# Head norms of two attention branches: squares summed as a rounded part and a remainder

## The reference, cut to what matters

```python
def rms_norm(x, g):
    xf = x.astype(jnp.float32)
    y = xf * lax.rsqrt(jnp.mean(xf * xf, axis=-1, keepdims=True) + EPS)
    return (y * g.astype(jnp.float32)).astype(x.dtype)

# in hybrid_layer, run for two layers; 4 heads of 64 in each branch
na = merge_heads(neighbourhood_attention(rms_norm(split_heads(nq, NA_HEADS), na_q_norm_g),
                                         rms_norm(split_heads(nk, NA_HEADS), na_k_norm_g),
                                         split_heads(nv, NA_HEADS), na_rpb))
mk, mv = jnp.split(rms_norm(mem, norm_mem_g) @ w_mem_kv, 2, axis=-1)
mo = merge_heads(memory_attention(rms_norm(split_heads(mq, MEM_HEADS), mem_q_norm_g),
                                  rms_norm(split_heads(mk, MEM_HEADS), mem_k_norm_g),
                                  split_heads(mv, MEM_HEADS)))
```

## Time and profile before

| What | Value |
|---|---|
| median of 3 runs | 3020.45 us (3017.92 to 3021.84) |
| the profiled execution's own time | 3013.83 us |
| its span in the profile | 3012.0 us |
| busy: PE, DVE, ACT, POOL | 98%, 44%, 23%, 72% of the span |

### The profile page before, as it was taken

The page is one execution under the profiler, slowest core; times in us unless marked ns, Lnnn a source line. Parts: engine busy times, 40 slices in busy tenths (PEclk is TensorE's granted clock), DMA queues, the critical chain, the costliest instruction groups (busy, mean ns, idle before and its releaser), DMA issues.

```text
span 3012.0 us, 43162 instructions
## 1 busy us (share of the span) xinstructions
PE 2948.2 (98%) x13960; PEld 2377.1 (79%) x13960; DVE 1339.8 (44%) x2200; ACT 682.4 (23%) x1366; POOL 2171.7 (72%) x3010
## 2 busy tenths in 40 slices
PE   9999999999999999999999999999999999999998
PEld 7768888888877688888887777788887777888886
DVE  6753243122565532553345765522236775431223
ACT  5321111010234211210102444410012333320101
POOL 8557777787975577787888655587777446787875
PEclk9999999999999999999999999999999999999999
DMA  5222223222332122322224222122222112222222
GB/s 188 70 71 91 98 91 114 98 96 94 104 132 71 64 98 98 108 98 93 100 94 138 105 80 67 66 97 96 98 98 98 64 64 84 92 98 96 94 97 91
DMA packets 80902, 285.78 MB, mean 95 GB/s; under 512 B 8720, under 2 KB 9616, under 8 KB 79472
## 3 DMA queue, kind: packets, MB, share of 16 engines
q1 hardware_dynamic: 76432, 266.65, 26.3%
q10 hardware_dynamic: 4320, 17.11, 1.6%
HBM read 279.20 MB, written 4.33 MB: 94 GB/s over the span
## 4 chain that ended last, share of the span: by engine, by line
PE 89%; DVE 7%; ACT 3%; issue 1%; DMA 0%; DVEq 0%; SPq 0%; ACTq 0%
PE pd L722 40%; PE pa L722 40%; PE pd L1015 2%; PE po L1056 1%; ACT work L192 1%; PE pa L777 1%; PE pa L1027 1%; DVE pair L204 1%; DVE work L200 1%; DVE t L204 1%; PE pd L1078 1%; DVE qk L196 0%; DVE qk L204 0%; PE pa L824 0%; ACT pair L192 0%
## 5 line engine op out<-in xcount | busy, mean ns | idle before, releaser
L668 POOL TENSOR_TENSOR w_lo<-w_raw,w_hi 128x256 fp32r<-128x256 f32 x2004 | 1543.7, 801 | 41.8
L663 POOL TENSOR_SCALAR w_hi<-w_raw 128x512 fp32r<-128x512 f32 x1002 | 629.7, 647 | 771.3 <-PE pa L722 431.8
L722 PE MATMUL pa<-h_hi,w_hi 128*128 128x512 f32 (+1 forms) x1912 | 755.0, 395 | 8.1 <-DVE t L204 5.7
L722 PE MATMUL pa<-h_hi,w_lo 128*128 128x512 f32 (+1 forms) x1912 | 743.5, 389 | 0.0
L722 PE MATMUL pa<-h_lo,w_hi 128*128 128x512 f32 (+1 forms) x1912 | 743.2, 389 | 0.0
L722 PEld LDWEIGHTS pa<-h_hi,w_hi 128*128 128x128 f32 x1912 | 360.2, 188 | 109.4 <-issue 28.7
L722 PEld LDWEIGHTS pa<-h_hi,w_lo 128*128 128x128 f32 x1912 | 360.0, 188 | 74.4
L722 PEld LDWEIGHTS pa<-h_lo,w_hi 128*128 128x128 f32 x1912 | 360.4, 188 | 73.0 <-issue 1.9
L722 PE MATMUL pd<-b_hi,w_hi 128*128 128x512 f32 x992 | 390.3, 393 | 8.4 <-DVE x_res L196 2.9
L722 PE MATMUL pd<-b_hi,w_lo 128*128 128x512 f32 x992 | 387.4, 391 | 0.0
L722 PE MATMUL pd<-b_lo,w_hi 128*128 128x512 f32 x992 | 387.1, 390 | 0.0
(11 more groups left out here) (220 smaller groups left out, 3100.7 us busy)
## 6 DMA issues: line engine op xcount, KB each, us to landing
w_raw<-in_w SPq DMA_DIRECT2D x501, 512.0 KB, 3.2
mrg<-in_nabias ACTq DMA_DIRECT2D x2, 2048.0 KB, 10.1
x_res<-in_x SPq DMA_DIRECT2D x8, 256.0 KB, 5.8
mrg<-in_mem ACTq DMA_DIRECT2D x2, 1024.0 KB, 4.9
kept_mem<-m_hi ACTq DMA_DIRECT2D x2, 1024.0 KB, 5.3
out_y<-mrg ACTq DMA_DIRECT2D x8, 256.0 KB, 2.1
mrg<-in_mem SPq DMA_DIRECT2D x1, 1024.0 KB, 8.8
vbuf<-in_count ACTq DMA_DIRECT2D x2, 512.0 KB, 3.3
```

What stands on the lines that cost most here:

```text
L663: ins = nc.gpsimd.tensor_scalar(w_hi[:, j, half], raw[:, j % RR, half], 1.0, 1.0, ALU.mult, ALU.mult)
L668: ins = nc.gpsimd.tensor_tensor(w_lo[:, j, part], raw[:, j % RR, part], w_hi[:, j, part].bitcast(F32), ALU.subtract)
L722: ins = mm(out, a, b, start=(first and k == 0 and e == 0), stop=(last and k == k_n - 1 and e == 2))
```

## The change

Each of the sixteen sums is made from a rounded part and a remainder. ACT squares as before and then copies the square into `sq_hi`, rounded. DVE subtracts: `sq_lo` is the square less `sq_hi`, written over the square. PE sums both with two rounded products by `ones_r`, a rounded copy of `blockones`, in place of one full-width product. The four sums of the retention's norm (Es) stay as they were. `sq_hi` takes the place in memory of `qs`, and `sq_lo` that of `sq`.

On DVE the subtractions stand at the beginning of the step that follows the one which made the query or key (`split_squares` in `piece` and in the tile steps). That of na0 Cq stands in mem1 Nk. The next step of DVE starts behind the subtraction, which waits for ACT's copy. Ahead of the first step of the first layer, DVE makes `ones_r` once.

```diff
-            def square_sum(k_n, mat, width=S, bank=None):
+            def square_sum(width=S, bank=None, split=True):
                 bank = bank or bank_a()
...
+                i = n.take("sq_used")
+                if split:
+                    pe.wait_ge(sq_split, n.take("sq_split") + 1)
+                    mm(bank[:, 0:width], ones_r[:, :], sq_hi[:, i % 2, 0:width], start=True, stop=False)
+                    ins = mm(bank[:, 0:width], ones_r[:, :], sq_lo[:, i % 2, 0:width], start=False, stop=True)
...
+            def square(src, width=S, split=True):
                 i = n.take("sq_used")
                 act.wait_ge(sq_used, n.free("sq_used", i, 2))
-                f(sq[:, i % 2, 0:width], src, ACT.Square).then_inc(sq_full, 1)
+                ins = f(sq[:, i % 2, 0:width], src, ACT.Square)
+                if split:
+                    chain(ins)
+                    f(sq_hi[:, i % 2, 0:width], sq[:, i % 2, 0:width], ACT.Copy).then_inc(sq_rounded, 1)
...
+            def squared(width=S):
+                n.to_split.append((n.take("sq_used") % 2, width))
+
+            def split_squares():
+
+                for slot, width in n.to_split:
+                    dve.wait_ge(sq_rounded, n.take("sq_split") + 1)
+                    v.tensor_tensor(sq_lo[:, slot, 0:width], sq[:, slot, 0:width],
+                                    sq_hi[:, slot, 0:width].bitcast(F32), ALU.subtract).then_inc(sq_split, 1)
+                n.to_split = []
...
             def piece(ph, p, what):
+                split_squares()
                 if what in ("Cq", "Ck"):
                     if ph.kind in ("na", "mem"):
                         rooted(qbuf[:, ph.q_slot(p, 0)] if what == "Cq" else kbuf[:, ph.k_slot(p, 0)],
                                ph.kind == "na")
+                        if (ph.kind, p, what) != ("na", 0, "Cq"):
+                            squared()
...
                     of_memory(kbuf[:, p, 0:MEM], rm_a)
+                    squared(MEM)
...
                     wide = MEM if ph.kind == "mem" else S
+                    if (ph.kind, p) == ("mem", 1):
+                        squared()
+                        split_squares()
                     head_normed(kbuf[:, ph.k_slot(p, 0), 0:wide], ph.params["k"], wide)
...
                         piece(ph, p, a)
                         continue
+                    split_squares()
                     j, blocks = ph.tiles[a]
...
                 if l == 0:
+                    dve.wait_ge(mats_in, 16)
+                    chain(v.tensor_copy(ones_r[:, :], blockones))
                     dve.wait_ge(rope_in, 16)
```

More of the change, by code:

```diff
@@ L462, in build @@
         mrg = sb("mrg", [P, KT, S])
+        with nc.sbuf_tensor("sq_lo", [P, 2, S], F32R) as sq_lo:
+            pass
         sq = sb("sq", [P, 2, S])
+        ones_r = sb("blockones_rounded", [P, P], F32R)
         rx = sb("rx", [P, S])
         pair2 = sb("pair2", [P, 2, S])
+        with nc.sbuf_tensor("sq_hi", [P, 2, S], F32R) as sq_hi:
+            pass
         qs = sb("qs", [P, 2, S])
@@ L537, in build @@
         sq_full, sq_used = sem("sq_full"), sem("sq_used")
+        sq_rounded, sq_split = sem("sq_rounded"), sem("sq_split")
         qk_full = sem("qk_full")
@@ L817, in _ @@
             n.begun = []
-            def square_sum(k_n, mat, width=S, bank=None):
+            def square_sum(width=S, bank=None, split=True):
                 bank = bank or bank_a()
[L821 to L825, removed]
+                i = n.take("sq_used")
[3 more added lines that the diff above has]
+                    ins = mm(bank[:, 0:width], ones_r[:, :], sq_lo[:, i % 2, 0:width], start=False, stop=True)
+                else:
+                    pe.wait_ge(sq_full, n.take("sq_full") + 1)
+                    ins = mm(bank[:, 0:width], blockones, sq[:, i % 2, 0:width], start=True, stop=True)
+                ins.then_inc(sq_used, 1)
             def wait_splits():
@@ L951, in piece @@
                         bank = bank_a()
-                        n.inside.append(lambda: square_sum(1, blockones, wide, bank=bank))
+                        n.inside.append(lambda: square_sum(wide, bank=bank))
                     else:
-                        square_sum(1, blockones, wide)
+                        square_sum(wide)
                 elif what == "Tv":
@@ L1096, in beside_ret @@
                 elif what == "Es":
-                    square_sum(1, blockones)
+                    square_sum(split=False)
                 elif what == "E":
@@ L1357, in take_a @@
                 return i
-            def square(src, width=S):
+            def square(src, width=S, split=True):
                 i = n.take("sq_used")
                 act.wait_ge(sq_used, n.free("sq_used", i, 2))
-                f(sq[:, i % 2, 0:width], src, ACT.Square).then_inc(sq_full, 1)
+                ins = f(sq[:, i % 2, 0:width], src, ACT.Square)
+                if split:
+                    chain(ins)
+                    f(sq_hi[:, i % 2, 0:width], sq[:, i % 2, 0:width], ACT.Copy).then_inc(sq_rounded, 1)
+                else:
+                    ins.then_inc(sq_full, 1)
             def root(out, size, width=S, k_n=1):
@@ L1646, in beside_ret @@
                     act.wait_ge(pv_done, n.at("pv_done", n.ret_end[p]))
-                    square(po[p][:, :])
+                    square(po[p][:, :], split=False)
                     head_root(None)
@@ L2257, in beside_ret @@
                     n.squares[p] = n.take("pa_done")
+                    n.take("sq_used")
                 elif what == "E":
```

## The result

The changed kernel takes 3040.32 us (median of 4, 3037.74 to 3042.21), the kernel before on the same chip 3019.23 (4 runs, 3017.92 to 3021.84): 1.0069 times as long, with an interval of 1.0056 to 1.0081. That is 21 us more, where the prediction's sum had 13.9, and it lies 0.3 us above the upper end of the range. Direction and places were right, the size was not.

The account below looks back on a forecast made before the run. It took PE to bound the kernel up to the first neighbourhood key's sum and DVE behind it, in both hybrid layers. Site delays of 8.2 + 5.7 = 13.9 us, added to the median 3020.45, gave 3034.3 us, range 3027 to 3040.

Parts of the forecast that it names:

- the prediction's sum: Site delays of both hybrid layers, 8.2 us in the first and 5.7 in the second: 13.9 us more.
- The mechanism by site: Delays worked out norm by norm in both hybrid layers; site sum as worked out 3030 to 3036.5 us, chance 0.60.
- The way to each sum: Square, copy, gaps and subtraction from DVE's product to its subtraction's end: 2.3 us wide, 1.7 us for 256 columns.
- G is pushed back: Second neighbourhood query: DVE's G step starts behind the subtraction, 2.3 us more in each layer.
- the root: Second neighbourhood key: ACT's copy stands between square and root, 0.7 us more in each layer.
- the foretold places: PE waits at the first layer's memory queries, about 2.6 us, and inside the first neighbourhood key's linear, 2.6 and 3.1.
- the one at the key's sum: First neighbourhood key, first layer: PE finishes its linear at 67.3 us, waits again, and the sum ends at 68.8.
- PE's saving: Rounded products save PE 0.40 us per wide sum and 0.20 per narrow one, 5.6 us in all.
- hidden splits: Rival: subtractions end before PE comes, as at the first neighbourhood query's sum; only PE's saving remains, 3014.9 us; chance 0.05.
- the last two sites absorbed: Rival: each layer's 3.0 us in G and the last key vanish in DVE's existing waits, 3028.4 us; chance 0.12.
- a delay at its end is passed on whole: Behind the norm stretch PE waits for almost nothing, 0.4 us at longest up to 200 us, so delay carries through.
- The clock rival: Clock falls in the new stalls inside the linear or the longer idle stretch: 3 us more, 3037.3 us; chance 0.18.

## Why the prediction was right, and where it was wrong

**Right.** The mechanism by site. The way to each sum is as long as worked out (idle of 1.42 us ahead of the subtraction, 0.69 to 1.03 for it), G is pushed back by 2.1 (11.1 less 9.0) and the root by 0.3 more (0.7 were worked out), and the waits stand at the foretold places but for the one at the key's sum. In the second layer the sites come to 6.0 us, against 5.7; that is in part luck, since the delay grows there by only 0.3 us up to the first reduction (1.0 was worked out), and the slower linear (9.12 us), which the sum has at full speed, makes up for it. PE's saving gives nothing in time, as the run with the rounded part alone shows most plainly. The rivals with hidden splits, and with the last two sites absorbed, fall.

**The step that failed: "a delay at its end is passed on whole".** It was read from the short waits behind 108 us: PE hardly waits there, so PE sets the time and the rest follows it. The chain says otherwise. In the first layer of the kernel before DVE sets the time up to the transposes of the second neighbourhood values as well (132.9 us), just in step with PE; in its second layer PE came last there, 0.6 us behind the end of DVE's product (934.32 against 933.74). Split layers fall nearly always into the case in which DVE's normalisations run beside POOL and last twice as long; unsplit layers did so in 2 of 9. PE then waits some 3 us, and the linear behind the wait runs in part at the lower clock (7.29 us instead of 5.46). So the delay is not passed on whole: in the profiles 5.2 us are added to it behind the first layer's norms, and none with less work for DVE. Since the kernel before loses such time in some executions too, less of it is left between the medians: the pair of runs with less work puts it at 3.5 us of the 21 (21.1 less 17.6), an estimate within their noise. Why a split shifts PE, and with it POOL, against DVE in just this way is only argued. PE does come to the transposes only 10.9 us late (143.44 against 132.56), sooner than the root's 11.4 would have it; a reason would be that in the changed kernel the clock falls in the one wait for T (4.54 us) and is back at 0.98 from 111 us, when the next linear starts, while in the kernel before that linear ran at 0.50 and 0.77.

**Mis-sized terms, first layer.** The reduction of the first scores is 6.05 us late and not 3.6, the first neighbourhood key's sum 9.0 (72.54 against 63.58) and not 5.2, the root 11.4 and not 8.2. Some 0.7 of the missing 3.2 us are there at the memory queries' sums already, which end 3.3 us late (38.90 against 35.60) and not 2.6. The rest is of two kinds, side by side: the split of the first memory key, for which nothing was charged, and the clock, which the sum has at full speed throughout. Kept clock and that key undone together give some 4 us, 1.9 of them up to the first scores.

**The clock rival** (3037.3, chance 0.18) was right in its mechanism: the clock fell to the lower level behind the wait of 2.20 us (which followed one of 1.18) and behind the lone ones of 3.12 and 3.17, and 33 matmuls took 1.6 us longer. The warning of idle gaps that the prediction cited from the Trainium skill (TensorE: Matmul & The Clock Gate, "Why this matters for your kernels") thus holds here for gaps that stand alone. But the rival was priced as if a slower PE were felt in full, and while the first memory key was split as well, most of it was not.

**The sum.** Where 13.9 were worked out for the sites, the two first profiles have 17.4, with the clock and the first memory key in it, and the pair with less work for DVE 17.5 (10.9 in the first layer and 6.6 in the second). That leaves some 3.6 of the 21 for the stretch behind the norms. The clock and the first memory key are settled together, not one by one.

**The base.** The profiled execution of the kernel before was one in which the normalisations of neither layer were long (medians of 355 and 353 ns), 5 to 7 us under the medians of its runs. A difference of one trace from another holds such luck; 28.4 us would have been read where 21 is typical.

## What to carry to other kernels

Short waits of the busiest engine don't show that it sets the time: an engine that delivers just in time does so too, and the chain must be followed until it truly leaves that engine before a delay is said to be passed on. A step that takes work off one engine and puts a wait at the head of another's queue costs what stands behind that head; before such a change is given up, move the step in the order, which was worth 9 of 21 us here. And where two delays may lie side by side, undo both at once, since each alone may look cheap.

## What was not expected of the hardware

DVE's 128 x 256 normalisation takes 0.35 us alone and up to 0.93 beside POOL's splitting of weights. It goes one way or the other in one unchanged kernel, from execution to execution. With less work for DVE the kernel before is 4 us faster but varies nearly as much (3012.81 to 3019.78 in 11 runs, 3014.25 to 3024.49 in 15 of the kernel before beside it), so what else moves its time stays open.
